# Attention with another order of query tiles in its second half

## The reference, cut to what matters

```
for q0 in range(0, s, Q_BLOCK):          # 4 blocks of 128 queries
    q1 = q0 + Q_BLOCK
    qb, kb, vb = q[:, :, q0:q1], k[:, :, :q1], v[:, :, :q1]
    sc = einsum("bhqd,bhkd->bhqk", qb, kb) * scale
    p = softmax(where(mask, sc, -inf))   # 16 heads of 64
    a = p[:, :, 0] - lam * p[:, :, 1]    # 8 pairs of heads
    outs.append(einsum("bhqk,bhkd->bhqd", a, vb))
o = rmsnorm(concatenate(outs), sub_norm) * (1.0 - lambda_init)
return o @ w_o
```

## Time and profile before

| | |
|---|---|
| median of 3 runs | 1914.59 us (1914.56 to 1914.89) |
| the profiled execution, its own time | 1916.84 us |
| its span, first to last instruction | 1915.1 us |
| PE busy | 1894.5 us (99%) |
| DVE busy | 804.5 us (42%) |
| ACT busy | 717.3 us (37%) |
| POOL busy | 550.2 us (29%) |
| mean granted TensorE clock | 0.999 |

### The profile page before, as it was taken

The page is one execution under the profiler, slowest core; times in us unless marked ns, Lnnn a source line. Parts: engine busy times, 40 slices in busy tenths (PEclk is TensorE's granted clock), DMA queues, the critical chain, the costliest instruction groups (busy, mean ns, idle before and its releaser), DMA issues.

```text
span 1915.1 us, 29430 instructions
## 1 busy us (share of the span) xinstructions
PE 1894.5 (99%) x11978; PEld 1643.2 (86%) x11978; DVE 804.5 (42%) x1240; ACT 717.3 (37%) x1124; POOL 550.2 (29%) x332
## 2 busy tenths in 40 slices
PE   9999999999999999999999999999999999999998
PEld 7888788888888887887679999999999877888887
DVE  6465552200000006866741110110101776999996
ACT  5332232332222224357640001000000655878785
POOL 4466663365545544423321002010010200200000
PEclk9999999999999999999999999999999999999999
DMA  9523223233233332311119989888888678999993
GB/s 345 184 78 98 68 95 102 79 110 99 89 103 96 94 112 68 109 45 45 56 40 399 362 314 337 288 303 294 313 300 296 234 289 310 412 403 395 377 391 145
DMA packets 283562, 396.21 MB, mean 207 GB/s; under 512 B 12737, under 2 KB 190913, under 8 KB 283425
## 3 DMA queue, kind: packets, MB, share of 16 engines
q1 hardware_dynamic: 279488, 381.67, 56.7%
q0 software_dynamic: 3936, 12.62, 1.6%
HBM read 374.48 MB, written 21.08 MB: 207 GB/s over the span
## 4 chain that ended last, share of the span: by engine, by line
PE 95%; DVE 1%; ACT 1%; issue 1%; DVEq 0%; DMA 0%; ACTq 0%; POOLq 0%; SPq 0%
PE ps L2200 17%; PE ps L2207 8%; PE ps L2264 6%; PE ps L2266 6%; PE ps L2265 6%; PE ps L425 6%; PE ps L426 6%; PE ps L427 6%; PE ps L443 3%; PE ps L444 3%; PE ps L445 3%; PE ps L572 2%; PE ps L574 2%; PE ps L573 2%; PE ps L460 1%; PE ps L461 1%
## 5 line engine op out<-in xcount | busy, mean ns | idle before, releaser
L1306 POOL TENSOR_TENSOR w_lo<-raw,w_hi 128x1024 fp32r<-128x1024 f32 (+2 forms) x193 | 386.3, 2017 | 346.9 <-ACT w_hi L1001 346.8
L2051 DVE TENSOR_TENSOR s_lo<-s_raw,s_hi 128x1024 fp32r<-128x1024 f32 x264 | 318.7, 1246 | 42.8 <-ACT s_hi L2465 35.9
L2465 ACT ACTIVATE s_hi<-s_raw 128x1024 fp32r<-128x1024 f32 x264 | 272.9, 1060 | 62.7 <-PE ps L2266 43.0
L1001 ACT ACTIVATE w_hi<-raw 128x1024 fp32r<-128x1024 f32 x158 | 163.4, 1043 | 188.1 <-PE ps L445 115.7
L2808 DVE TENSOR_TENSOR hid<-ps,silu_g 128x160 f32<-128x160 f32 x88 | 28.5, 324 | 411.3 <-ACT silu_g L2425 411.2
L425 PE MATMUL ps<-act_a_hi,w_hi 128*128 128x512 f32 x512 | 199.6, 390 | 0.0
L426 PE MATMUL ps<-act_a_lo,w_hi 128*128 128x512 f32 x512 | 199.3, 389 | 0.0
L427 PE MATMUL ps<-act_a_hi,w_lo 128*128 128x512 f32 x512 | 199.2, 389 | 0.0
L2589 POOL TENSOR_TENSOR sum_rows<-sum_rows,y_rows_sb 128x1024 f32<-128x1024 f32 (+1 forms) x12 | 28.6, 2386 | 582.9 <-ACT y_rows_sb L2430 319.7
L2425 ACT ACTIVATE silu_g<-ps 128x160 f32<-128x160 f32 x88 | 26.7, 303 | 449.0 <-PE ps L2200 440.2
L2200 PE MATMUL ps<-xT,w_gate 128*128 128x132 f32 x1408 | 173.4, 276 | 1.2 <-issue 0.8
(11 more groups left out here) (464 smaller groups left out, 3157.4 us busy)
## 6 DMA issues: line engine op xcount, KB each, us to landing
w_gate<-in_moe_w_gate SPq DMA_DIRECT2D x44, 1024.0 KB, 5.2
w_up<-in_moe_w_up SPq DMA_DIRECT2D x44, 1024.0 KB, 8.3
w_down<-in_moe_w_down SPq DMA_DIRECT2D x44, 1024.0 KB, 10.3
s_raw<-in_moe_w_gate SPq DMA_DIRECT2D x44, 1024.0 KB, 9.4
s_raw<-in_moe_w_up SPq DMA_DIRECT2D x44, 1024.0 KB, 9.8
s_raw<-in_moe_w_down SPq DMA_DIRECT2D x44, 1024.0 KB, 9.5
raw<-in_even_w_in SPq DMA_DIRECT2D x42, 512.0 KB, 3.8
raw<-in_attn_w_qkv SPq DMA_DIRECT2D x24, 512.0 KB, 3.7
```

What stands on the lines that cost most here:

```text
L1001: act.activation(w_hi[:, u % HL_SLOTS, 0:size(u)], raw[:, u % RAW_SLOTS, 0:size(u)], ACT.Copy).then_inc(hi_done, 1)
L1306: ins = pool.tensor_tensor(w_lo[:, u % HL_SLOTS, cut], raw[:, u % RAW_SLOTS, cut], flat(w_hi[:, u % HL_SLOTS, cut]), ALU.subtract)
L2051: return eng.tensor_tensor(s_lo[u % S_HL][:], s_raw[u // 2 % S_RAW][:, u % 2, :], s_hi[u % S_HL][:].bitcast(F32), ALU.subtract)
L2465: act.activation(s_hi[u % S_HL][:], s_raw[q % S_RAW][:, u % 2, :], ACT.Copy).then_inc(s_high, 1)
```

## The change

The second half of the heads takes the tiles of queries in the order 2, 3, 1, 0; `TILES[half]` holds the order and `TILES[1]` also orders `norm_o`, `turn_o`, `high_o`, `low_o`, `out_piece` and `add_out`. The items of a tile stay together: 16 to 19 are tile 2, 20 to 23 tile 3, 24 to 27 tile 1, 28 to 31 tile 0. The pieces of v keep their steps. ScalarE's `keep_v` of steps 19 and 23 is moved from behind `keep_diffT` to ahead of it; in step 23 `high_o(0, 0)` stays ahead of both.

```diff
+    TILES = ((0, 1, 2, 3), (2, 3, 1, 0))
+    items = [(pair, i) for half in range(2) for i in TILES[half] for pair in range(4 * half, 4 * half + 4)]
...
-                mm = pe.transpose(ps[:, turn_bank(j, half), b * P:(b + 1) * P], o_tok[:, j, c:c + P], ident[:])
+                mm = pe.transpose(ps[:, turn_bank(j, half), b * P:(b + 1) * P], o_tok[:, TILES[1][j], c:c + P], ident[:])
...
-            u, tt = U_WO + i, j
+            u, tt = U_WO + i, TILES[1][j]
...
             if 0 <= j < NT and at in (0, 2) and n < N - 1:
                 high_o(j, at // 2)
+            if n in (19, 23):
+                keep_v(value_piece(n)[0], value_piece(n)[2])
             if n < N + 2:
                 keep_diffT(n - 2)
...
-            if value_piece(n) and value_piece(n)[1] == 3:
+            if value_piece(n) and value_piece(n)[1] == 3 and n < 16:
                 keep_v(value_piece(n)[0], value_piece(n)[2])
...
-            pool.wait_ge(o_sq, 4 * half + i + 1)
-            c = 8 * i + 4 * half
+            pool.wait_ge(o_sq, 4 * half + j + 1)
+            c = 8 * TILES[half][j] + 4 * half
...
-            tt = j
-            dve.wait_ge(o_rms, 4 * half + j + 1)
+            tt = TILES[1][j]
+            dve.wait_ge(o_rms, 4 * half + j + 1 if half else tt + 1)
```

More of the change, by code:

```diff
@@ L249, in build_trunk @@
     hT_last, router_ready, lgT_done, lgT_kept = sem("hT_last"), sem("router_ready"), sem("lgT_done"), sem("lgT_kept")
-    items = [(pair, i) for half in range(2) for i in range(NT) for pair in range(4 * half, 4 * half + 4)]
+    TILES = ((0, 1, 2, 3), (2, 3, 1, 0))
+    items = [(pair, i) for half in range(2) for i in TILES[half] for pair in range(4 * half, 4 * half + 4)]
     N = len(items)
@@ L1226, in high_o @@
             act.wait_ge(turned, 8 * 3 + 2 * j + half + 1)
-            cut = slice(j * P, (j + 1) * P)
+            cut = slice(TILES[1][j] * P, (TILES[1][j] + 1) * P)
             act.activation(act_a_hi[:, 4 * half:4 * half + 4, cut],
@@ L1385, in _, with roots_of_heads @@
         low_parts(U_WO - 1)
-        def roots_of_heads(half, i):
-            pool.wait_ge(o_sq, 4 * half + i + 1)
-            c = 8 * i + 4 * half
+        def roots_of_heads(half, j):
+            pool.wait_ge(o_sq, 4 * half + j + 1)
+            c = 8 * TILES[half][j] + 4 * half
             pool.tensor_scalar(head_ss[:, 32 + c:36 + c], head_ss[:, c:c + 4], P * EPS, None, ALU.add)
@@ L1807, in add_out @@
                 dve.wait_ge(unit_used, U_WO + 4)
-            xx = x_sb[:, j, 0:512]
+            xx = x_sb[:, TILES[1][j], 0:512]
             dve.tensor_tensor(xx, ps[:, bank, :], xx, ALU.add).then_inc(acc_evac, 1)
```

## The result

The changed kernel is slower: 1920.29 us (median of 8 runs, 1918.54 to 1921.72) against 1914.72 us for the kernel before (8 runs, 1914.28 to 1915.32). The ratio is 1.003, with a 95% interval of 1.0021 to 1.0038: +5.6 us, +0.3%. The profiled execution took 1921.72 us, its span is 1920.0 us and its mean granted clock 0.997 (before: 1916.84, 1915.1 and 0.999). The added lines shift those of the kernel: `scores` is L600, `turn_diff` L614, `heads` L627, `turn_o` L640, `out_piece` L657 to L659, `keep_v` L1177, `keep_heads` L1787.

A forecast was written before the change was run, and what follows sets the result against it. The prediction took the kernel as bound by TensorE, 99% busy, so only its waits could change. New waits of 9.9 us less 6.3 us of old ones gave +3.6 us on 1914.59: 1918.2 us, range 1914.0 to 1920.6 us.

The forecast's parts named there:

- the forecast's own case: Two waits at the v copies and a tail no better than before: 1916.6 to 1920.2 us, chance 0.71.
- The waits at the copies: TensorE waits for v copies ahead of `heads(16)` in step 19, 1.84 us, and `heads(20)` in step 23, 2.96 us.
- `norm_o` beside GpSimd: Step 23: `norm_o` slowed beside GpSimd's low parts, 0.2 us added; up to 0.6 us higher if unlucky.
- Steps 16 to 18 and 24 to 27 without waits: TensorE has no wait in steps 16 to 18 and almost none in steps 24 to 27.
- The tail: Last narrow tiles: thinner work covers three remaining chains, leaving waits of 2.5, 1.7 and 0.7 us.
- Behind `turn_diff(29)`: Tail: copy-out chain makes TensorE wait 2.0 us, then `out_piece(2, 0)` 0.46 us more for `add_out(1)`; together 2.5 us.
- Behind `turn_diff(31)`: Tail: low part needed by `out_piece(2, 2)` is covered only by two `heads` of 0.14 us; wait 1.7 us.
- steps 28 to 31: Waits of 0.37 us behind `turn_o(1, 1)`, 0.14 at `out_piece(1, 0)`, 0.22 at `turn_o(2, 0)`; together 0.7 us.
- The sum: Over the second half's loop: new waits 9.9 us less old waits 6.3 us, +3.6 us.
- the flat 0.22 us: Added to each of 11 old waits beside wide tiles, on 3.85 us idle, making 6.3 us of old waits.
- Rivals 1 and 2: No new tail waits, 1913.3 us, chance 0.16; copies also cheap at 1.7 us, 1910.0 us, chance 0.06.
- Rival 3, the clock: Clock falls to 1.2 GHz in step 23's long wait, costing 4 us more: 1922.2 us, chance 0.07.

The follow-up runs named there:

- Experiment 4: Changed kernel with the second half's `heads` reading the first half's values, so none waits for a v copy: loop 66.01 us, only the loop comparable.
- experiment 3: Changed kernel with filler matmuls in one place each: 12 in step 23 alone, 1918.61 us; 7 and 4 in the tail alone, 1919.59 us.
- the filled and swapped version: Changed kernel with `keep_heads` and `add_out` ahead of `low_o` on VectorE, plus 12, 3 and 4 filler matmuls: 1918.41 us.
- the filled one: Changed kernel with 23 useless filler matmuls in TensorE's waits, 12 in step 23 and 11 in the tail: first 1919.35 us, repeated 1920.23 us.
- experiment 5: Changed kernel with the two v copies back behind `keep_diffT` in steps 19 and 23: 1921.41 us, ratio 1.0036.
- experiment 1: Changed kernel with 12 filler matmuls ahead of `heads(20)`, 7 ahead of `heads(29)`, 4 behind `heads(31)`: 1919.35 us, loop 68.15 us.
- experiment 2: Changed kernel with the same 23 filler matmuls in step 23 and the tail, run and profiled a second time: 1920.23 us, loop 68.08 us.
- the filler of step 23: Changed kernel with only the 12 filler matmuls ahead of `heads(20)`, none in the tail: 1918.61 us, ratio 1.0023.

## Why the prediction was right in its sum and wrong at the clock

The forecast was 1918.2 us with a range of 1914.0 to 1920.6; 1920.29 is inside, near its upper end, and 0.1 us above the forecast's own case (1916.6 to 1920.2). That it is inside is partly luck: the range left out a fall of the clock, the clock did fall, and only its smaller price kept the time under 1920.6. By chances I had put 0.50 on "same" and 0.43 on "slower", with the border at 0.2%; at +0.3% it is slower.

- **The waits at the copies: right.** Forecast 1.84 and 2.96 + 0.2, measured 1.80 and 3.04 us. The chain is the one forecast. ScalarE's rows, the copy right behind `exps` in step 19 and behind `exps` and `high_o` in step 23:

```profile
903.05 0.60 ACT L1177 ACTIVATE v_tok<-ps 128x512 f32<-128x512 f32 x1
...
920.35 0.69 ACT L1229 ACTIVATE act_a_hi<-ps,small 128x512 fp32r<-128x512 f32 x1
920.93 0.59 ACT L1177 ACTIVATE v_tok<-ps 128x512 f32<-128x512 f32 x1
```

- **`norm_o` beside GpSimd: right in size.** VectorE's rows give it 917.55 - 916.79 = 0.76 us, 0.16 more than the 0.60 of a free one; I had added 0.2. GpSimd's low parts ran beside it (914.50 to 918.22), and it didn't lose the whole 0.8 us of one of them, which I had named as the worst case.

```profile
916.79 0.84 DVE L1795 TENSOR_TENSOR o_tok<-o_tok,head_ss 128x512 f32<-128x512 f32 x1
917.55 1.21 DVE L1768 TENSOR_REDUCE soft<-ps 128x2 f32<-128x1024 f32 x1
```

- **Steps 16 to 18 and 24 to 27 without waits: right.** The trace has none there; what looks slow in step 24 is the clock.
- **The tail: right in place, somewhat too large.** Behind `turn_diff(29)` it lost 950.94 - 948.59 - 0.36 = 1.99 us (forecast 2.0), but only 0.29 for the output piece (forecast 0.46, a term for which the prediction shows no row). Behind `turn_diff(31)` it lost 0.70 + 0.75 = 1.45 (forecast 1.7). In steps 28 to 31 it lost 0.48, all ahead of `heads(27)` (forecast 0.7 in three places; the 0.14 and 0.22 of the other two had no row either, and no wait came there).
- **The sum: right, with two errors that cancel.** The new waits are 1.80 + 3.04 + 2.28 + 1.45 + 0.48 = 9.05 us, not 9.9. Counted place by place, by the same distances of starts, the old ones are 5.3 us (of 0.27 to 1.19 us, in nine places), not 6.3: the flat 0.22 us that I added for each of 11 waits counted too much. The difference is 3.75, against 3.6 forecast and the 3.85 of the loop with the clock held. That the two errors were of one size (0.85 and 1.0 us) is luck.
- **Rivals 1 and 2: wrong.** The waits of tail and copies all came. Experiment 4 shows besides that even free copies would not have made the order faster (+0.1 to +0.2 us in the loop, not -1.3): a wait of 1.10 us takes their place.
- **Rival 3, the clock: this is the step that failed.** The forecast says "the clock at 1.00" and gives its fall a chance of 0.07 at +4 us. It falls in the profiled run twice, for some 1.5 us each (1.44 and 1.54 in experiment 3), and by the single times, as argued there, once or more in 7 of 8 runs. The price for one fall was too high, since I let all of step 24 run at half speed; the chance was far too low; and the second place, the tail, I didn't see at all. There the longest wait is 1.3 us, but from 948.59 to 951.45 TensorE has two transposes and four `heads` matmuls to do, 0.66 us of work in 2.86. The Trainium skill (TensorE: Matmul & The Clock Gate, Part 1) tells of a kernel whose TensorE idled briefly but often between groups of matmuls, and whose clock went back and forth between its two levels. The trace agrees for the tail, where the clock went to 0.63 and 0.51 behind short waits. The prediction named the page and then gave it too little weight.

So of the median's +5.6 us about 3.7 to 3.9 are waits (the filled and swapped version's 3.25 + 0.4, the filled one's loop 3.85), and the rest, 1.7 to 1.9, is what the clock takes: one fall in most runs, two in some. That the falls of the unprofiled runs are those of the profiled ones is argued from times and mean clocks, not shown. The order of the tiles is no gain because the tail's waits replace those of the wide tiles, and the copies of v come on top, since tile 2 and tile 3 of v are now needed in the step in which they are made.

## What to carry to other kernels

Before a step is moved ahead, look for what is made just in time for it: an order that puts the consumer of the last piece first pays the whole chain from PSUM through the copy, here twice. In a kernel whose TensorE is 99% busy, a wait can cost more than its length when it is long or stands among thin work, so read the granted clock in short stretches of the trace around every new wait, and behind every late load too, not its mean over the span. And if single times fall into levels, look for what is as large as the distance of the levels before explaining the median: here a fall of the clock (1.5 us) and late weights (1.6 us) are alike in size, and a mean clock of three digits tells them apart only roughly.

## What the runs showed of the hardware

- A wait of 1.64 us in step 19 left the clock alone, one of 2.08 us in the same place (experiment 5) was followed by 0.50; waits of 2.89 and 3.38 us were followed by 0.50. At the first expert weights a wait of 1.97 us left it at 1.00 (experiment 1) and one of 2.12 us was followed by 0.58 and 0.57 (experiment 2). The ones of 0.23 and 1.32 us with three small matmuls around them were followed by 0.50 in three profiles (the changed kernel, experiment 4, the filler of step 23) and not in that of experiment 5.
- A fall costs 1.5 us (1.44, 1.54, and 3.05 for two in the loop; 1.58 at the expert weights). Each matmul of an output piece takes 0.43 us from start to start in place of 0.23.
- Twelve useless 128-wide matmuls in a wait of 3 us keep the clock and don't lengthen the wait (3.48 us both ways).
- The first expert weights can land 1.6 us later behind the same issues (first expert matmul 7.7 to 8.1 us behind the first issue in ten profiles, 9.5 and 9.6 in the two of the filled kernel). The cause stays open.
